# Four edits to a hybrid transformer trunk: x by column halves, expert 0 ranked alone, weight quarters between 32-row products, a reordered last round

## What is computed

```python
for i in range(2):
    mix = gated_deltanet(h, ...) if i == 0 else stick_breaking_attention(h, ...)
    h = layer_norm(alpha * h + mix)
    ff = swiglu(h, ...) if i == 0 else moe_swiglu(h, ...)
    h = layer_norm(alpha * h + ff)

# gated_deltanet: proj = x @ w_in (k, q, z, v columns); per head and chunk of 64 tokens
T = triangular_solve(eye + L, eye)          # inverse of a unit lower triangle, 64x64

# moe_swiglu: each token goes to its two best of 8 experts
top_val, top_idx = lax.top_k(xt @ router, 2)
for e in range(8):
    y = y + combine[:, e:e+1] * ((silu(xt @ w_gate[e]) * (xt @ w_up[e])) @ w_down[e])
```

## Time and profile before

| | |
|---|---|
| median of three runs | 1476.69 us (1475.25 to 1477.11) |
| the profiled execution's own time | 1473.62 us |
| its span, first to last instruction | 1471.9 us |
| PE busy | 1439.4 us, 98% of the span |
| DVE, ACT, POOL busy | 841.2 (57%), 693.3 (47%), 118.0 us (8%) |
| DMA | 466.25 MB, mean 317 GB/s; 427 to 429 GB/s in most slices from slice 20 on |

### The profile page before, as it was taken

The page is one execution under the profiler, slowest core; times in us unless marked ns, Lnnn a source line. Parts: engine busy times, 40 slices in busy tenths (PEclk is TensorE's granted clock), DMA queues, the critical chain, the costliest instruction groups (busy, mean ns, idle before and its releaser), DMA issues.

```text
span 1471.9 us, 19078 instructions
## 1 busy us (share of the span) xinstructions
PE 1439.4 (98%) x7704; PEld 1066.5 (72%) x7704; DVE 841.2 (57%) x750; ACT 693.3 (47%) x686; POOL 118.0 (8%) x134
## 2 busy tenths in 40 slices
PE   9999999999999999999999899999899999999996
PEld 9899988888888899888843488834588633788432
DVE  6787666755444746799910399610698300998102
ACT  6755476343443346477700387400587201877001
POOL 1668110000000000004000000000000000000001
PEclk9999899999999999999999999999999999999999
DMA  8493327545555462599999999999999999999995
GB/s 294 130 346 107 108 86 281 206 173 204 201 192 194 149 208 94 226 363 391 374 428 428 427 427 427 427 428 428 429 429 427 424 427 428 428 430 427 424 426 225
DMA packets 78563, 466.25 MB, mean 317 GB/s; under 512 B 7572, under 2 KB 14248, under 8 KB 57000
## 3 DMA queue, kind: packets, MB, share of 16 engines
q1 hardware_dynamic: 75368, 459.00, 78.0%
q10 hardware_dynamic: 2336, 4.29, 0.8%
q0 software_dynamic: 800, 2.12, 0.4%
HBM read 455.93 MB, written 9.46 MB: 316 GB/s over the span
## 4 chain that ended last, share of the span: by engine, by line
PE 82%; POOL 5%; DMA 5%; DVE 5%; issue 2%; ACT 1%; POOLq 0%; SPq 0%; ACTq 0%; DVEq 0%
PE ps L1305 18%; PE ps L1307 17%; PE ps L1306 17%; PE ps L2043 16%; DMA ring_raw<-in_moe_w_gate 5%; POOL X L652 2%; POOL ab L647 2%; PE ps L1339 1%; PE ps L1341 1%; PE ps L1342 1%; PE ps L1948 1%; PE ps L1625 1%; PE ps L2001 1%; PE ps L1630 1%; PE ps L1936 1%
## 5 line engine op out<-in xcount | busy, mean ns | idle before, releaser
L2146 DVE TENSOR_TENSOR ring_low<-ring_raw,w_hi_more 128x2048 fp32r<-128x2048 f32 x84 | 190.1, 2287 | 52.2 <-ACT w_hi_more L1208 39.9
L2043 PE MATMUL ps<-ring_raw,xs_light 128*64 128x512 f32 (+1 forms) x1024 | 197.3, 540 | 0.0
L2146 DVE TENSOR_TENSOR ring_low<-ring_raw,w_lo_more 128x2048 fp32r<-128x2048 f32 x84 | 189.0, 2286 | 8.0 <-ACT w_lo_more L739 6.5
L2146 DVE TENSOR_TENSOR w_lo<-raw,w_hi 128x2048 fp32r<-128x2048 f32 x67 | 153.6, 2305 | 62.0 <-ACT w_hi L739 60.8
L1306 PE MATMUL ps<-ring_low,xeh 128*128 128x512 f32 x448 | 176.6, 394 | 0.0
L739 ACT ACTIVATE w_hi_more<-ring_raw 128x2048 fp32r<-128x2048 f32 x75 | 142.2, 1915 | 39.5 <-PE ps L1307 22.5
L739 ACT ACTIVATE w_lo_more<-ring_raw 128x2048 fp32r<-128x2048 f32 x75 | 143.0, 1917 | 35.5 <-PE ps L1307 31.2
L2043 PEld LDWEIGHTS ps<-ring_raw,xs_light 128*64 128x64 f32 x1024 | 72.1, 137 | 119.7 <-issue 111.0
L739 ACT ACTIVATE w_hi<-raw 128x2048 fp32r<-128x2048 f32 x66 | 124.6, 1911 | 40.9 <-PE ps L1342 28.7
L2864 DVE TENSOR_TENSOR hs<-hs,ps 128x512 f32<-128x512 f32 (+1 forms) x16 | 9.9, 619 | 188.1 <-PE ps L2043 188.1
L1305 PE MATMUL ps<-w_hi_more,xeh 128*128 128x512 f32 x224 | 91.0, 406 | 16.5 <-DVE ring_low L2146 16.2
(11 more groups left out here) (432 smaller groups left out, 2911.4 us busy)
## 6 DMA issues: line engine op xcount, KB each, us to landing
ring_raw<-in_moe_w_gate SPq DMA_DIRECT2D x56, 2048.0 KB, 14.0
ring_raw<-in_moe_w_up SPq DMA_DIRECT2D x56, 2048.0 KB, 12.9
ring_raw<-in_moe_w_down SPq DMA_DIRECT2D x56, 2048.0 KB, 15.3
raw<-in_gdn_w_in SPq DMA_DIRECT2D x23, 1024.0 KB, 5.9
raw<-in_ffn_w_gate SPq DMA_DIRECT2D x14, 1024.0 KB, 5.7
raw<-in_ffn_w_up SPq DMA_DIRECT2D x14, 1024.0 KB, 6.1
raw<-in_ffn_w_down SPq DMA_DIRECT2D x14, 1024.0 KB, 5.1
raw<-in_sb_w_in SPq DMA_DIRECT2D x12, 1024.0 KB, 5.7
```

The costliest lines, as they stand in the source:

```text
L2043: last = nc.tensor.matmul(ps[half * HALF:half * HALF + HALF, bank, 0:width], tile, raw_slot(j)[:, w], start=start, stop=False, skip_group_ ...
L2146: V.tensor_tensor(unit_lo(j), raw_slot(j), unit_hi(j).bitcast(F32), ALU.subtract).then_inc(lo_done, 1)
```

## The change

Four groups of edits; the reference's arithmetic stays as it is.

1. **x by halves.** x comes in four transfers: columns 0 to 511 of both token blocks ahead of unit 0, columns 512 to 1023 behind it. The transposes, ACT's copies and DVE's low parts of the second half move into unit 0 (PE: ahead of its last quarter; ACT: behind the four pieces of unit 0; DVE: behind `lo(0)`).
2. **Expert 0 ranked alone.** DVE makes a mask of expert 0 only (`above0`, `place0`, `mask0`), PE ranks by it (3 products). The comparison of all experts (`experts_placed`) moves behind `lo` of unit 5, PE's ranking products and totals (`counted`) into heavy round 0 behind the first `up`, and DVE's copies of them (`experts_counted`) to just ahead of `experts_ranked`.
3. **Quarters.** Each group of 64 small products is cut in two groups of 32 with a quarter of unit 19 (12 products) behind each. DVE's `lo(19)` moves ahead of its wait for POOL's last step.
4. **Last round.** The last pair of units becomes two single units with a semaphore each. The residual goes into the banks before `gate(3)`, both token blocks together. The output banks become (4, 5) and (0, 7) in place of (4, 5) and (6, 7).

```diff
+OUT_BANK = [(4, 5), (0, 7)]
...
-        R_pe = Stages(sem("R_pe"), ["lg", "rk", "tot"])
+        R_pe = Stages(sem("R_pe"), ["lg", "rk0", "rk", "tot"])
...
@@ SP
-            for t in range(NT):
-                sp.dma_start(X[:, t], x[0, t * P:(t + 1) * P, :]).then_inc(x_in[t], 16)
+            def half_in(half):
+                w = slice(512 * half, 512 * half + 512)
+                for t in range(NT):
+                    sp.dma_start(X[:, t, w], x[0, t * P:(t + 1) * P, w]).then_inc(x_in[half][t], 16)
+
+            half_in(0)
             for k in range(4):
                 sp.dma_start(raw_slot(0)[:, k * 512:k * 512 + 512], gdn_w_in[0, k * P:k * P + P, CHUNK_COL["k"]:CHUNK_COL["k"] + 512])\
                   .then_inc(first_in[k], 16)
+            half_in(1)
...
+            def last_units_in(r, u, w, e):
+                j = u + DOWN[3]
+                sp.wait_ge(unit_used, units(j + 1 - RING, FC * (r - 1)))
+                pair = weight_pair(w, e, 6)
+                sp.dma_start(raw_slot(j), pair[:, 0:UNIT]).then_inc(raw_sem(j), 16)
+                sp.dma_start(raw_slot(j + 1), pair[:, UNIT:2 * UNIT]).then_inc(last_unit_in, 16)
...
@@ ACT
-            for t in range(NT):
-                transposed(0, t, xT0h, (4, 6))
+            first_transposed(0)
...
                 nc.scalar.activation(unit_hi(0)[:, k * 512:k * 512 + 512], raw_slot(0)[:, k * 512:k * 512 + 512], ACT.Copy)\
                   .then_inc(first_hi, 1)
+            first_transposed(1)
             hi(1)
...
@@ PE, unit 0
                     if j == 0:
+                        if k == 3:
+                            first_transposed(1)
                         pe.wait_ge(first_hi, k + 1)
...
@@ PE
+            def quarter(j, m):
+                stationary(j, j % 2, CHUNK_BANK[j // 2], xT0h, xT0l, (m,))
...
-            unit(19, (0,))
+                quarter(19, p)
...
-            unit(19, (1,))
+                quarter(19, 2 + p)
...
-            pe.wait_ge(R_dve.sem, R_dve.after("mask"))
+            pe.wait_ge(R_dve.sem, R_dve.after("mask0"))
+            def ranked(bank, of):
+                lt, ones = counting[:, 0, :], counting[:, 1, :]
+                nc.tensor.matmul(ps[:, bank, 0:NE], lt, of[:, 0, :], start=True, stop=True)
+                nc.tensor.matmul(ps[:, bank, NE:2 * NE], lt, of[:, 1, :], start=True, stop=False)
+                return nc.tensor.matmul(ps[:, bank, NE:2 * NE], ones, of[:, 0, :], start=False, stop=True)
+            def counted():
+                pe.wait_ge(R_dve.sem, R_dve.after("mask"))
+                ones = counting[:, 1, :]
+                ranked(2, mask).then_inc(R_pe.sem, 1)
+                nc.tensor.matmul(ps[:, 3, 0:NE], ones, mask[:, 0, :], start=True, stop=False)
+                nc.tensor.matmul(ps[:, 3, 0:NE], ones, mask[:, 1, :], start=False, stop=True).then_inc(R_pe.sem, 1)
+            ranked(3, mask0).then_inc(R_pe.sem, 1)
...
@@ PE, heavy round
                 up(0)
+                if l is None:
+                    counted()
                 gate(1, (0, 1))
...
@@ PE, light round
+                if last_round:
+                    pe.wait_ge(x_added, NT * l + NT)
+                    residual(0)
+                    residual(1)
                 gate(3, range(2))
                 up(3)
-                pe.wait_ge(x_added, NT * l + NT)
-                if last_round:
-                    residual(0)
...
@@ DVE
             lo(0)
+            first_transposed(1)
             lo(1)
...
             v_scaled(1)
+            lo(19)
             dve.wait_ge(sub_step, 2 * (SUB - 1))
...
+            step("above0", V.tensor_tensor(rt["od"][:], rt["lg"][:], rt["lg"][:, :, 0:1].broadcast_to([P, NT, NE]), ALU.is_gt))
+            step("place0", V.tensor_reduce(rs["df"][:].rearrange("p t a -> p (t a)"), rt["od"][:], AX_X, ALU.add))
+            step("mask0", V.tensor_scalar(mask0[:], rs["df"][:].broadcast_to([P, NT, NE]), float(TOPK), None, ALU.is_lt))
...
             row_low(1, 1)
-            lo(U_MOE + 1)
-            step("rk", V.tensor_copy(ranks[:], rank))
-            dve.wait_ge(R_pe.sem, R_pe.after("tot"))
-            step("tot", V.tensor_copy(totals[:], ps[:, 3, 0:NE]))
...
+                if half == 0:
+                    lo(U_MOE + 1)
...
+            experts_placed()
...
                 if first:
+                    experts_counted()
                     experts_ranked()
```

More of the change, by code:

```diff
@@ L246, in hybrid_trunk @@
         counting = sb("counting", [P, 2, P], F32R, fm)
-        mask = sb("mask", [P, NT, NE], F32R, fm)
+        mask, mask0 = (sb(n, [P, NT, NE], F32R, fm) for n in ("mask", "mask0"))
         ranks = sb("ranks", [P, NT, NE], F32, fm)
@@ L304, in hybrid_trunk @@
         xh_done, xl_done = sem("xh_done"), sem("xl_done")
-        x_in = [sem(f"x_in{t}") for t in range(NT)]
+        x_in = [[sem(f"x_in{half}{t}") for t in range(NT)] for half in range(2)]
         small_in, late_in = sem("small_in"), sem("late_in")
@@ L359, in hybrid_trunk @@
             sem(n) for n in ("later_done", "capped", "prob_done", "prob_cut", "mixed", "mixed_hi", "mixed_lo"))
-        R_pe = Stages(sem("R_pe"), ["lg", "rk", "tot"])
+        R_pe = Stages(sem("R_pe"), ["lg", "rk0", "rk", "tot"])
         R_act = Stages(sem("R_act"), ["rwh", "lt", "ones", "ex"])
-        R_dve = Stages(sem("R_dve"), ["rwl", "z", "bf", "ba", "bb", "bc", "nl", "lr", "hr", "lg", "above", "same", "first", "both", "place", "mask",
[1 row of a table removed]
+        R_dve = Stages(sem("R_dve"), ["rwl", "z", "bf", "ba", "bb", "bc", "nl", "lr", "hr", "lg", "above0", "place0", "mask0",
+                                      "far", "at0", "pick0", "pick1", "above", "same", "first", "both", "place", "mask", "rk", "tot", "oh1", "oh2", "od", "ol", "df", "key", "less",
                                       "pos", "hv", "b2", "bl", "cap", "ov", "ovb", "ovp", "ob", "oo", "oa", "pa", "pb", "st",
@@ L782, in load_ln, with first_transposed @@
                 act.dma_start(row[:, 1, :], ln_b[k // 2, k % 2].partition_broadcast(P)).then_inc(ln_in, 16)
-            for t in range(NT):
-                transposed(0, t, xT0h, (4, 6))
+            def first_transposed(half):
+                for t in range(NT):
+                    act.wait_ge(xt_pe, 2 * half + t + 1)
+                    nc.scalar.activation(xT0h[:, 4 * half:4 * half + 4, t * P:(t + 1) * P],
+                                         ps[:, 4 + 2 * t + half, :].rearrange("p (k s) -> p k s", s=P),
+                                         ACT.Copy).then_inc(xt_hi, 1)
+            first_transposed(0)
             def first_tap(n):
@@ L1330, in stationary_high_first, with stationary @@
                 last.then_inc(unit_used, 1)
-            def stationary(j, half, bank, xh, xl, part):
+            def stationary(j, half, bank, xh, xl, ms):
                 pe.wait_ge(lo_done, units(j))
-                for m in range(2 * part[0], 2 * part[-1] + 2):
+                for m in ms:
                     o = ps[:, bank + m // 2, (m % 2) * SEQ:(m % 2 + 1) * SEQ]
@@ L1432, in _, with first_transposed @@
             pe.wait_ge(cst_step, CST_IDENT)
-            for t in range(NT):
-                for half in range(2):
-                    transpose_x((4, 6)[t] + half, t, half, x_in[t], 16)
+            def first_transposed(half):
+                for t in range(NT):
+                    transpose_x((4, 6)[t] + half, t, half, x_in[half][t], 16)
+            first_transposed(0)
             def unit(j, part=(0, 1)):
@@ L1466, in unit @@
                 else:
-                    stationary(j, half, bank, xT0h, xT0l, part)
+                    stationary(j, half, bank, xT0h, xT0l, range(2 * part[0], 2 * part[-1] + 2))
+            def quarter(j, m):
+                stationary(j, j % 2, CHUNK_BANK[j // 2], xT0h, xT0l, (m,))
             def k_to_tokens(i):
@@ L2018, in heavy_round @@
                 up(1)
-                if l is not None:
+                if l is None:
+                    pe.wait_ge(R_dve.sem, R_dve.after("tot"))
+                else:
                     pe.wait_ge(y_copied, r)
@@ L2648, in _ @@
             other = rt["lg"][:].unsqueeze(2).broadcast_to([P, NT, NE, NE])
-            V.tensor_tensor(above[:], other, mine, ALU.is_gt).then_inc(R_dve.sem, 1)
-            step("same", V.tensor_tensor(same[:], other, mine, ALU.is_equal))
-            step("first", V.tensor_tensor(same[:], same[:], before[:].unsqueeze(1).broadcast_to([P, NT, NE, NE]), ALU.mult))
-            step("both", V.tensor_tensor(above[:], above[:], same[:], ALU.add))
-            step("place", V.tensor_reduce(rt["place"][:], above[:], AX_X, ALU.add))
@@ L2675, in _, with experts_counted @@
                  .then_inc(K_dve.sem, 1)
-            for k in range(2, 5):
+                if half == 0:
+                    lo(U_MOE + 1)
+            for k in range(2, 6):
                 lo(U_MOE + k)
-            lo(U_MOE + 5)
+            experts_placed()
+            def experts_counted():
```

(4 more changed lines are left out.)

67 lines of the change are left out of this document (37 added, 30 removed), and 1 row of the table R_dve.

## The result

| | before | after |
|---|---|---|
| median of 21 runs | 1473.93 us (1469.86 to 1477.11) | 1480.91 us (1475.51 to 1490.09) |
| ratio to before | | 1.0052 (1.0041 to 1.0063) |
| profiled execution, its span | 1473.62, 1471.9 us | 1484.78, 1483.0 us |

The forecast was -1.6 us, and 1471.6 to 1479.4 for the time; the ratio makes it +7.7 us, and the median lies above the range. The forecast's 1475.1 was counted from a median of three runs (1476.69); the median of the 21 is 2.8 lower. The spread of the changed kernel is twice that of before.

A forecast was written before the change was run, and what follows sets the result against it. PE was taken to bound ahead of the router, DMA transfers in the second half. Terms +0.2 + 2.1 - 3.9 + 0 = -1.6 against a median of 1476.69 gave 1475.1 us, range 1471.6 to 1479.4.

The forecast's parts named there:

- `lo(19)` moves into DVE's 4.90 us of waiting for POOL and costs nothing: Part 3, DVE's wait ending at 138.32: the 2.2 us low part of unit 19 is hidden there, cost 0.
- The prediction's price without cover: Part 3: the early low part of unit 19 would cost 2.2 us if DVE's wait did not hide it.
- The loss to the clock is 4.53 us: Part 3, PE from 140.73 to 160.25: 19.52 us against 14.99 at full clock; gain taken as -3.9.
- No group is longer than 2.1 us ..., this keeps the clock: Part 3's main assumption: short small-product groups with 1.44 us of full products between keep full clock; ends -4.5 and 0.
- the clock falls all the same: Third rival, 15%: half rate returns or comes for another reason, part 3 gives 0; +2.3, 1479.0 us.
- The rule that I weighed against part 3: Clock falls after PE idles on a wait; with PE always at work, part 3 would be worth 0.
- the working on DVE: Part 2, heavy round 0: added DVE steps and copies make `sloti` and the scatters 2.45 us later.
- SP's release: Part 2, SP's wait for the token scatters: release moves from 703.22 to 705.3, end +2.1; ends 0 and +2.6.
- its rival: Part 2, second rival, 22%: the scatters' delay is not on the path; -3.7 in all, 1473.0 us.
- its ends: Part 1, start of the kernel: x by halves costs +0.2 us, with ends -0.6 and +0.6.
- I let ACT decide: Part 1, units 0 and 1: ACT's two copies of 0.51 us ahead of `hi(1)` set the pace; +0.2 us.
- 0 as forecast: Part 4, last round: PE has no idle time to fill, so 0; ends -0.5 and +0.5.

The follow-up runs named there:

- the early low part alone: Kernel before with only the low part of unit 19 moved ahead of DVE's wait for POOL's last step: ratio 1.003, +3.6 ± 0.5 us.
- The quarters without the wait: Kernel before with unit 19 in quarters and its low part between DVE's two transposes: ratio 1.0, +0.9 ± 0.9 us; whole change with that order: 1.0005.
- Part 4 alone: Kernel before with only the last-round edits (single units, residual ahead of gate 3, other output banks): ratio 1.0008, +0.7 ± 0.5 us.
- part 2 alone: Kernel before with only expert 0 ranked alone and the full comparison and ranking moved later: ratio 1.0, -0.2 ± 0.6 us.
- The three kernels with a wait of 1.8 us ahead of the block: Against before: whole change +7.9 us; quarters plus early low part of unit 19 +4.9 us; that early low part by itself +3.6 us.
- two kernels without the wait: Changed kernel without quarters and early low part, +2.1 ± 0.7 us; kernel before with only x by halves, +2.1 ± 0.8 us.
- The alternating kernel: Kernel before with the two halves of each group of 64 small products alternating head by head: ratios 0.9986 and 0.9982, -2.4 ± 0.3 us.

## Why the prediction was wrong, step by step

- **Part 3, "`lo(19)` moves into DVE's 4.90 us of waiting for POOL and costs nothing": this step failed.** The wait was seen as room for DVE. But the engine waited for is POOL, and POOL's step runs as long as DVE's pass over the unit does (2.39 us against 0.46). The room was on the path. The Trainium skill ("GPSIMD Engine Reference", "Specifications") says that GpSimd shares its SBUF interfaces with VectorE and contends with DVE instructions of two SBUF inputs. The trace agrees: the subtraction has two, and I had not weighed it, nor the eight stretched steps in the trace of before. The prediction's price without cover was 2.2 us; measured is +3.6 ± 0.5 for the early low part alone, +0.2 ± 0.7 when it stands between the transposes, and moving it there in the whole change takes that from +7.9 to +0.3.
- **"The loss to the clock is 4.53 us", the gain of part 3: mis-sized, and this step failed too.** The quarters without the wait gain nothing that can be measured (+0.9 ± 0.9 alone, +0.3 ± 0.7 in the whole change). The sum for full clock, 14.99 us from the first group to the third kind, is right. But the block as it stood before runs at full clock in some executions by itself. Part 4 alone, whose block is unchanged, PE and then the stretch:

```profile
141.62 4.13 PE L1597 MATMUL ps<-zs,tt 32*32 32x32 f32 x128
148.75 4.13 PE L1606 MATMUL ps<-X,ab 32*32 32x32 f32 x128
156.75 2.21 PE L1614 MATMUL ps<-ab,X 32*32 32x32 f32 x64
```

```profile
141.60:156.70 15.10, 15.08 (x312) 14.74 (x312) 13.70 (x18) 5.95 (x5) 11.71 (x7) 1.00 0.22 72
```

From the first group to the third kind it takes 15.13 us; part 2 alone takes the same; with quarters at full clock it is 16.03. The five profiles of this block with its low part where it was have 10.2 (before), 13.6, 0, 10.2 and 0 us at half clock in it, none behind a wait of PE. So a fall that the quarters could save was there in some executions only. My estimate of its mean: before has 30.5 us at half clock over 127 executions and the two profiles without a fall in the block 26.5, which leaves 4 us for the block and not 10; at 0.33 to 0.44 us for each (the slope, and 4.53 / 10.2) that is 1.3 to 1.8 us.

- **"No group is longer than 2.1 us ..., this keeps the clock": it did so only where PE does not wait, as far as the profiles go.** Without the wait two profiles of quarters have the block at 1.00, third kind at 157.2 (forecast 156.3, before 160.25). With the wait, ahead of the block or in it, it fell in all four profiles that have quarters in this form, for 7 to 24 us. The rival that took the place of the forecast is the third, "the clock falls all the same"; it allowed for another cause and did not name it. The rule that I weighed against part 3 is the Trainium skill's ("TensorE: Matmul & The Clock Gate", Part 1, "HAM oscillation"), that the clock falls after idle waits. The trace agrees in part. The three kernels with a wait of 1.8 us ahead of the block have 34.4 to 39.9 us at half clock in the mean, and each has less when one line takes the wait away (30.4, 28.7 and 28.0); but the clock also falls behind no wait at all, as above, and two kernels without the wait have 33.7 and 34.4. I had set the rule aside on the rows of before, and did not ask whether the change brings such a wait.
- **Part 2: the working on DVE was right (+2.41 against 2.45), and SP's release nearly so.** By the forecast it came 76.0 us behind the start of round 0, 3.05 later than before; the five profiles with part 2 have 74.7 in the mean, the 13 without it 71.9, so +2.8. What was mis-sized lies around it: round 0 starts 1.21 earlier (forecast 0.97), and 0.7 of the delay is made up between the release and round 2, which comes 2.1 later against the start of round 0. That leaves +0.9 at round 2 against the forecast's 2.1. In the time of the part not even that shows (-0.2 ± 0.6), as its rival had it.
- **Part 1: the size is inside its ends, the reason was wrong.** POOL's first step of the chain, a mark on the way, is at 85.85 us in the mean of the five profiles with part 1 (85.45 to 86.05) and at 85.42 in the 13 without (84.96 to 85.90): +0.43, forecast +0.2, ends -0.6 and +0.6. I let ACT decide and counted its copies; but PE waits 0.4 to 1.0 us for unit 1 in each profile with part 1, and ACT ahead of it for unit 1's transfer, which is issued behind two more issues of SP. The count of issues on SP's queue was left out.
- **Part 4: 0 as forecast,** within the error.

Added up, the parts alone give +2.1 - 0.2 + 4.9 + 0.7 = +7.5, the whole +7.9.

What stays open: why the clock falls in one execution and not in the next, and whether it is the wait as such or the place in time to which it moves the block. The changed kernel's +7.9 is more than its wait (1.9) and its 9.4 us more at half clock (3.1 at the rate of 0.33) account for, and part 1's share of the rest is open too. The alternating kernel has a wait of 1.73 us inside the block and no more time at half clock than before (28.8); no run here tests why.

## What to carry to other kernels

Idle time in front of a wait is free only if the work put there does not slow the engine that is waited for; look at what that engine does while the first one is busy elsewhere in the trace. Here the trace of before had the answer eight times. Where a gain hangs on the granted clock, size it over many executions, not from one profile; and it is safer to keep waits of PE away from stretches of small products. A transfer cut in two costs one more issue on the queue (two took 0.91 us here), which delays those behind it even when the bytes are the same.

## What the hardware showed unexpectedly

- A POOL step that met a DVE subtraction of 128x2048 took 2.39 us in place of 0.46, and ended within 0.4 us of it, in each profile of the early low part; the eight such meetings in the trace of before took 2.35 to 2.81.
- Products of 32x32 in two row groups of PE's array overlap when they alternate: 64 in 2.2 us against 4.1, with no other change.
- At half clock 32 small products took 3.62 us against 2.21 at full clock.
- The same block ran at full clock throughout in two executions and had 10 to 14 us at half clock in three, with PE at work all the time in each.
